# Strict decay sums on VectorE, and the chunk state from the pairing keys, in a bidirectional RWKV-7 recurrence

## The reference, cut to what matters

```python
def step(state, inp):
    r_t, w_t, k_t, v_t, a_t, b_t = inp
    sa = jnp.einsum('bhvk,bhk->bhv', state, a_t)
    state = state * w_t[:, :, None, :] + sa[..., None] * b_t[:, :, None, :] + v_t[..., None] * k_t[:, :, None, :]
    return state, jnp.einsum('bhvk,bhk->bhv', state, r_t)
```

## Time and profile before

| | |
|---|---|
| median of three runs | 1738.15 us (1738.0 to 1738.5) |
| profiled execution | span 1738.9 us from the first to the last instruction; no other time of it is given |
| TensorE busy | 1681.4 us (97%), weight loads 1105.9 us (64%) |
| VectorE, ScalarE, GpSimd busy | 837.8, 333.1 and 221.8 us |
| layer 1 and the mixing inputs | 0 to 589 us |
| prologue of the recurrence | 589 to 655.5 us, TensorE busy 64.1 of 66.5 |
| first turn (group 0, prepares 1) | 655.5 to 712.8 us, TensorE 54.8 of 57.3, VectorE 39.8, GpSimd 24.1 |
| second turn | 712.8 to 772.7 us, TensorE 54.8 of 59.9, VectorE 45.8, GpSimd 35.0 |
| third turn | 772.7 to 833.8 us, TensorE 56.2 of 61.1, VectorE 43.6, GpSimd 26.8 |
| last turn, output projection, router | 833.8 to 868 us |
| experts | 868 to 1738.9 us, TensorE 851 of 870.9, DMA 95% busy, 400 GB/s |

### The profile page before, as it was taken

One profiled execution on the slowest core, in us unless ns is written; L12 is line 12 of the kernel. 1 busy time (PEld: TensorE's weight loads), 2 busy tenths in 40 slices (PEclk: granted clock), 3 DMA queues, 4 the chain that ended last, 5 costly groups with the idle time before them and its releaser, 6 DMA issues.

```text
span 1738.9 us, 31942 instructions
## 1 busy us (share of the span) xinstructions
PE 1681.4 (97%) x13592; PEld 1105.9 (64%) x13592; DVE 837.8 (48%) x1889; ACT 333.1 (19%) x721; POOL 221.8 (13%) x301
## 2 busy tenths in 40 slices
PE   8999998999999999899899999999999999999997
PEld 5888886688644558788856555555555555555553
DVE  6666663555648446867335233433333333343332
ACT  3234323112101225444220000000101000000000
POOL 1431340000001423642300000000000000000000
PEclk9999999999999999999999999999999999999999
DMA  8542427454642010100686999999999999999996
GB/s 307 215 145 97 151 92 242 145 188 151 212 145 97 25 31 23 32 15 17 249 320 269 387 387 426 428 426 426 426 427 427 426 426 426 427 427 426 427 427 251
DMA packets 111553, 460.47 MB, mean 265 GB/s; under 512 B 28064, under 2 KB 57008, under 8 KB 89776
## 3 DMA queue, kind: packets, MB, share of 16 engines
q1 hardware_dynamic: 109360, 457.60, 66.4%
q10 hardware_dynamic: 2048, 0.78, 0.2%
HBM read 456.26 MB, written 2.10 MB: 264 GB/s over the span
## 4 chain that ended last, share of the span: by engine, by line
PE 87%; DMA 5%; DVE 4%; ACT 2%; issue 1%; SPq 1%; POOL 0%; DVEq 0%
PE ps L1658 20%; PE ps L845 15%; PE ps L1027 12%; PE ps L899 10%; PE ps L1631 10%; PE ps L1668 6%; DMA arena<-mw 4%; PE ps L1638 3%; PE ps L853 2%; PE ps L1195 2%; PE ps L891 1%; PE ps L1555 1%; PE ps L1041 1%; PE ps L919 1%; PE ps L1309 1%
## 5 line engine op out<-in xcount | busy, mean ns | idle before, releaser
L1658 PE MATMUL ps<-arena 128*64 128x256 f32 x3584 | 397.7, 380 | 5.3 <-DMA arena<-mw 5.3
L1658 PEld LDWEIGHTS ps<-arena 128*64 128x64 f32 x3584 | 256.7, 137 | 159.2 <-issue 30.7
L845 PE MATMUL ps<-arena 64*128 64x128 f32 (+13 forms) x1914 | 305.4, 329 | 15.2 <-DMA arena<-td 3.4
L2977 DVE TENSOR_TENSOR arena<-arena,ps 64x256 f32<-64x256 f32 x140 | 59.5, 425 | 460.0 <-ACT arena L2145 460.0
L845 PEld LDWEIGHTS ps<-arena 128*128 128x128 f32 (+4 forms) x1914 | 221.6, 187 | 83.2 <-issue 58.1
L1027 PE MATMUL ps<-arena 128*128 128x256 f32 x952 | 210.7, 379 | 0.1
L1631 PE MATMUL ps<-arena 128*64 128x512 f32 x896 | 203.0, 597 | 4.3 <-DMA arena<-mw 2.6
L1027 PEld LDWEIGHTS ps<-arena 128*128 128x128 f32 x952 | 178.5, 190 | 23.8 <-issue 0.5
L899 PE MATMUL ps<-arena 128*128 128x256 f32 (+1 forms) x714 | 189.0, 425 | 0.0
L2145 ACT ACTIVATE arena<-ps 64x256 f32<-64x256 f32 x140 | 52.7, 376 | 680.3 <-PE ps L1658 589.7
L899 PEld LDWEIGHTS ps<-arena 128*128 128x128 f32 x714 | 134.8, 190 | 50.6 <-issue 34.4
(11 more groups left out here) (288 smaller groups left out, 1377.9 us busy)
## 6 DMA issues: line engine op xcount, KB each, us to landing
arena<-mw SPq DMA_DIRECT2D x167, 2048.0 KB, 27.0
arena<-wqkv SPq DMA_DIRECT2D x35, 1024.0 KB, 7.3
arena<-fw SPq DMA_DIRECT2D x32, 1024.0 KB, 7.2
arena<-wrkv SPq DMA_DIRECT2D x12, 1024.0 KB, 7.4
arena<-awo SPq DMA_DIRECT2D x4, 1024.0 KB, 6.3
arena<-bwo SPq DMA_DIRECT2D x4, 1024.0 KB, 8.6
arena<-mw SPq DMA_DIRECT2D x2, 1024.0 KB, 38.6
arena<-rows SPq DMA_DIRECT2D x4, 384.0 KB, 4.8
```

The costliest lines, as they stand in the source:

```text
L845: last = mm(o, a, b, start=(n == 0), stop=(n == len(pairs) - 1))
L1658: last = mm(ps[r, g % 4, 0:256], picked[:, b, k, 0:64], w[:, k, a * 256:(a + 1) * 256], start=(k == 0), stop=(k == KB - 1))
L2977: dve.tensor_tensor(hid_e[RH:P, p % 2, i, :], sg_e[RH:P, j % 2, :], ps[RH:P, bank, 0:256], ALU.mult).then_inc(hide_sb, 1)
```

## The change

The full sums of both tiles come from one matmul of 128x512 per direction. The strict sums are the full ones minus `sig`: VectorE subtracts them (`strict_sums`) straight out of PSUM into `E[:, :, 1]`, and ScalarE takes their exponential in place in one operation (`strict_powers`). `powers` shrinks to two exponentials of 128x512 and the one of two columns. `ends`, `end_powers` and `to_end` are gone: `state` sums from the same scaled keys that the pairings use, and the factor that carries them to the chunk's end is now part of `pm`, whose two columns are each made by two matmuls of one column that add up. Since `state` reads these keys a turn later, the scaled keys alternate between two places, at the size that `keb` had. In VectorE's list of a turn `scaled_b` now stands ahead of `scaled_a`, and for direction 1 one step of the chain of the solve earlier; `scaled_a` of direction 1 stands one step later.

```diff
@@ -330,11 +330,11 @@
         cross = m.take(BLK // 2, BLK // 2)
-        keb0 = [m.take(2, RQ) for _ in range(2)]
+        spare_kt = [m.take(T, RQ) for _ in range(2)]
         b0 = m.take(T, RQ)
...
         b_ = [b0, m.take(T, RQ)]
-        keb = [keb0, [m.take(2, RQ) for _ in range(2)]]
+        spare_inv = [m.take(T, RQ) for _ in range(2)]
         y_sum = m.take(T, RQ)
@@ -359,6 +359,8 @@
             dirs.append(o)
+        k_at = [[o["kt"] for o in dirs], spare_kt]
+        b_at = [[o["inv"] for o in dirs], spare_inv]
         ar_early = [lent12.take(2, 2, P) for _ in range(2)]
@@ -779,7 +781,7 @@
             for d in range(2):
-                sp.wait_ge(ke_ok[d], 2 * NQ)
+                sp.wait_ge(ops_ok[d], 4 * NQ)
             for n in range(U_BWO):
@@ -1237,20 +1239,14 @@
             def cumulated(q, d):
+
                 pe.wait_ge(za.sb, q * 4 + 2 * d + 2)
-                cen = [const[:, C_CEN + (2 * d + n) * P:C_CEN + (2 * d + n + 1) * P] for n in range(2)]
-                for t in range(T):
-                    for n in range(2):
-                        last = run(ps[:, 2 * d + t, n * RQ:(n + 1) * RQ], [(cen[n], dirs[d]["sig"][:, t, :])])
-                last.then_inc(cum_ps, 1)
-
-            def ends(q, d):
-
                 sig = dirs[d]["sig"]
-                pe.wait_ge(ex_ok[d], q * 6 + 2)
-                run(ps[:, 2 * d, 0:RQ], [(tri(LS if d == 0 else US), sig[:, d, :])])
+                run(ps[:, 2 * d, :], [(const[:, C_CEN + 2 * d * P:C_CEN + (2 * d + 1) * P], sig.rearrange("p t n -> p (t n)"))]).then_inc(cum_ps, 1)
                 for pr in range(2):
-                    last = run(ps[:, 2 * d, RQ + pr:RQ + pr + 1], [(sig[:, 1 - d, pr * P:(pr + 1) * P], const[:, C_HALF + d:C_HALF + d + 1])])
+                    c = slice(pr * P, (pr + 1) * P)
+                    last = run(ps[:, 2 * d + 1, pr:pr + 1], [(sig[:, d, c], const[:, C_HALF + 1 - d:C_HALF + 2 - d]),
+                                                             (sig[:, 1 - d, c], const[:, C_HALF + d:C_HALF + d + 1])])
                 last.then_inc(end_ps, 1)
             def operands(q, i):
@@ -1259,10 +1255,10 @@
                 if i < 2:
-                    pe.wait_ge(ex_ok[i], q * 6 + 6)
+                    pe.wait_ge(ex_ok[i], q * 4 + 4)
                 else:
                     pe.wait_ge(X.sb, at_set(q, i - 2))
-                for done, bank, first, second in ((tA, b, o["E"][:, t, 1], o["E"][:, t, 0]), (tB, b + 1, o["inv"][:, t], o["kt"][:, t])):
+                for done, bank, first, second in ((tA, b, o["E"][:, t, 1], o["E"][:, t, 0]), (tB, b + 1, b_at[q % 2][d][:, t], k_at[q % 2][d][:, t])):
                     for pr in range(2):
@@ -1393,9 +1389,6 @@
                 four(z2, ETm[1], ze[1][0], RH)
-                if nq:
-                    ends(nq, 0)
-                    ends(nq, 1)
                 need(E2T, 0, 1)
@@ -1420,12 +1413,12 @@
                     for d in range(2):
-                        pe.wait_ge(ke_ok[d], 2 * (q + 1))
-                        k = keb[q % 2][d]
+                        pe.wait_ge(ops_ok[d], 4 * (q + 1))
+                        k, b = k_at[q % 2][d][:, d], b_at[q % 2][d][:, d]
                         for h in range(4):
...
                             at = (2 * d + h // 2) * RH
-                            last = run(ps[r, bank, at:at + RH], [(k[:, 0, c], value(q, d, h)), (k[:, 1, c], ze[d][0][:, h, :])])
+                            last = run(ps[r, bank, at:at + RH], [(k[:, c], value(q, d, h)), (b[:, c], ze[d][0][:, h, :])])
                     last.then_inc(St.ps, 1)
                 def keys_by_state(n, d):
@@ -1516,8 +1509,6 @@
             project(6)
-            ends(0, 0)
-            ends(0, 1)
             project(7)
@@ -1980,7 +1971,7 @@
                 if q:
-                    act.wait_ge(ke_ok[d], 2 * q)
+                    act.wait_ge(ops_ok[d], 4 * q)
                 for n, name in enumerate(("sig", "a")):
@@ -1988,15 +1979,17 @@
                 act.wait_ge(cum_ps, 2 * q + d + 1)
-                for t in range(T):
-                    act.activation(o["E"][:, t].rearrange("p a n -> p (a n)"), ps[:, 2 * d + t, :], ACT.Exp, scale=-DECAY).then_inc(ex_ok[d], 1)
-                    act.activation(o["inv"][:, t, :], ps[:, 2 * d + t, 0:RQ], ACT.Exp, scale=DECAY).then_inc(ex_ok[d], 1)
-
-            def end_powers(q, d):
-
+                sums = ps[:, 2 * d, :].rearrange("p (t n) -> p t n", t=T)
+                act.activation(b_at[q % 2][d], sums, ACT.Exp, scale=DECAY).then_inc(ex_ok[d], 1)
+                act.activation(o["E"][:, :, 0, :], sums, ACT.Exp, scale=-DECAY).then_inc(ex_ok[d], 1)
                 act.wait_ge(end_ps, 2 * q + d + 1)
-                act.activation(keb[q % 2][d][:, 1, :], ps[:, 2 * d, 0:RQ], ACT.Exp, scale=-DECAY).then_inc(ex_ok[d], 1)
-                act.activation(pm[q % 2][d], ps[:, 2 * d, RQ:RQ + 2], ACT.Exp, scale=-DECAY).then_inc(ex_ok[d], 1)
+                act.activation(pm[q % 2][d], ps[:, 2 * d + 1, 0:2], ACT.Exp, scale=-DECAY).then_inc(ex_ok[d], 1)
+
+            def strict_powers(q, d):
+
+                o = dirs[d]
+                act.wait_ge(excl_ok[d], q + 1)
+                act.activation(o["E"][:, :, 1, :], o["E"][:, :, 1, :], ACT.Exp, scale=-DECAY).then_inc(ex_ok[d], 1)
@@ -2048,9 +2041,9 @@
                 if nq:
+                    strict_powers(nq, 0)
                     powers(nq, 1)
-                    end_powers(nq, 0)
-                    end_powers(nq, 1)
+                    strict_powers(nq, 1)
                 at[0] = 12
@@ -2091,8 +2084,8 @@
             project_out(6)
-            end_powers(0, 0)
-            end_powers(0, 1)
+            strict_powers(0, 0)
+            strict_powers(0, 1)
             project_out(7)
@@ -2574,22 +2567,22 @@
             def scaled_a(q, d):
...
                 o = dirs[d]
-                dve.wait_ge(ex_ok[d], q * 6 + 4)
+                dve.wait_ge(ex_ok[d], q * 4 + 4)
                 dve.scalar_tensor_tensor(o["E"][:, :, 1, :], kkn, -1.0, o["E"][:, :, 1, :], ALU.mult, ALU.mult).then_inc(ops_ok[d], 1)
...
             def scaled_b(q, d):
+                o, b = dirs[d], b_at[q % 2][d]
+                dve.wait_ge(ex_ok[d], q * 4 + 1)
+                dve.tensor_tensor(k_at[q % 2][d], o["kd"], b, ALU.mult).then_inc(ops_ok[d], 1)
+                dve.tensor_tensor(b, o["a"], b, ALU.mult).then_inc(ops_ok[d], 1)
+
+            def strict_sums(q, d):
+
                 o = dirs[d]
-                dve.tensor_tensor(o["kt"], o["kd"], o["inv"], ALU.mult).then_inc(ops_ok[d], 1)
-                dve.tensor_tensor(o["inv"], o["a"], o["inv"], ALU.mult).then_inc(ops_ok[d], 1)
-
-            def to_end(q, d):
-
-                o, k = dirs[d], keb[q % 2][d]
-                dve.wait_ge(ex_ok[d], q * 6 + 6)
-                dve.tensor_tensor(k[:, 0, :], o["kd"][:, d, :], k[:, 1, :], ALU.mult).then_inc(ke_ok[d], 1)
-                dve.tensor_tensor(k[:, 1, :], o["a"][:, d, :], k[:, 1, :], ALU.mult).then_inc(ke_ok[d], 1)
+                dve.wait_ge(ex_ok[d], q * 4 + 2)
+                dve.tensor_tensor(o["E"][:, :, 1, :], ps[:, 2 * d, :].rearrange("p (t n) -> p t n", t=T), o["sig"], ALU.subtract).then_inc(excl_ok[d], 1)
@@ -2693,19 +2686,19 @@
                     keys(nq, 0)
-                    keys(nq, 1)
+                    key_rates(nq, 1)
+                    strict_sums(nq, 0)
+                    key_steps(nq, 1)
+                    scaled_b(nq, 0)
                     scaled_a(nq, 0)
-                    scaled_b(nq, 0)
                 chain_step(z2, 8, 0)
                 if nq:
-                    scaled_a(nq, 1)
+                    strict_sums(nq, 1)
+                    scaled_b(nq, 1)
                 chain_step(z3, 10, 0)
                 if nq:
-                    scaled_b(nq, 1)
+                    scaled_a(nq, 1)
                 chain_step(z5, 14, 0)
-                if nq:
-                    to_end(nq, 0)
-                    to_end(nq, 1)
                 dve.wait_ge(St.ps, q + 1)
@@ -2742,16 +2735,16 @@
             key_rates(0, 1)
+            strict_sums(0, 0)
+            strict_sums(0, 1)
             key_steps(0, 0)
+            scaled_b(0, 0)
             scaled_a(0, 0)
-            scaled_b(0, 0)
             key_steps(0, 1)
+            scaled_b(0, 1)
             scaled_a(0, 1)
-            scaled_b(0, 1)
             off_blocks(0, 0)
             off_blocks(0, 1)
-            to_end(0, 0)
-            to_end(0, 1)
             off_blocks(0, 2)
```

More of the change, by code:

```diff
@@ L464, in build @@
         ops_ok = [sem(f"ops_ok{d}") for d in range(2)]
-        ke_ok = [sem(f"ke_ok{d}") for d in range(2)]
+        excl_ok = [sem(f"excl_ok{d}") for d in range(2)]
         ex_ok = [sem(f"ex_ok{d}") for d in range(2)]
```

## The result

| | before | after |
|---|---|---|
| median, four runs each, same chip | 1738.33 us (1738.0 to 1741.33) | 1748.66 us (1747.74 to 1749.21) |
| ratio of the times, 95% interval | 1 | 1.0054 [1.0043, 1.0066] |
| span of the profiled execution | 1738.9 us | 1746.7 us |

A forecast was written before the change was run, and what follows sets the result against it. VectorE's list, stretched by GpSimd, was taken to bound z2 to z4 in two of three turns, TensorE elsewhere. Terms -1.4 + 0.4 + 3.9 + 3.4 = +6.3 us gave a 1744.5 us median, range 1738.5 to 1749 us.

The forecast's parts named there:

- stretched subtractions: Rival: in the second and third turn the subtraction and the extra operation cost 1.7 us each, not 0.6; 1748.9 us, chance 0.1.
- TensorE's savings: On TensorE, `cumulated` keeps its length and `ends` falls out: 1.77 us a turn, 7.1 us in all.
- Prologue: Before the first turn, the first transposes start earlier, limited by the scaled operands of direction 0; gain 1.4 us.
- First turn: z3 starts 0.9 us earlier, but work ahead of the z3 additions makes them 0.4 us later; net +0.4 us.
- z2 and z3 additions: VectorE, second and third turn: z2 additions 0.65 us late, z3 additions 1.95 us late; price 3.9 us for both turns.
- Stops and clock: Second and third turn: TensorE stops about 4.8 us before z3, 2 before z4; clock falls to half, 3.4 us more.
- eight exponentials: On ScalarE, eight exponentials of a direction's 1,794 columns become four of 1,538; the new wait costs nothing.
- Sum of the recurrence: Prologue, first turn, late additions and clock together: -1.4 + 0.4 + 3.9 + 3.4 = +6.3 us.
- The step that failed: Everything after the recurrence, the experts' weight stream included, only shifts with it, so the span becomes 1745.2 us.
- From span to median: The median lies 0.75 us below the profiled span of 1745.2 us, at 1744.5 us.
- late additions, but the clock holds: Rival: VectorE's additions come late in the second and third turn, but TensorE's clock stays up; 1740.5 us, chance 0.15.
- parts cancel: Rival: fewer late microseconds in the recurrence and half of the clock's price; 1738 to 1741.6 us, chance 0.1.

The follow-up runs named there:

- State_alone: The kernel before with only the change's second half (state from the pairing keys, no `ends` or `to_end`), strict sums still on TensorE; 1740.79 us, ratio 1.0009 to before.
- reorder_z2: The changed kernel with the chain's additions moved forward in VectorE's list, the z2 additions also ahead of the second subtraction; 1733.47 us, ratio 0.9972 to before.
- before_reorder: The kernel before with the chain's z2 and z3 additions moved forward in VectorE's list, old arithmetic kept; 1732.47 us, ratio 0.9954 to before.
- fill: The changed kernel with nine matmuls that compute nothing between z2 and z3 of the second and third turn; 1742.06 us, ratio 1.0017 to before.
- reorder_z2_pad: reorder_z2 plus 18 small matmuls that compute nothing and two waits in the last turn's TensorE stop; 1722.68 us, ratio 0.9901 to before.
- reorder: The changed kernel with the z2 and z3 additions moved forward in VectorE's list, behind both subtractions; 1735.77 us, ratio 0.9974 to before.

## Why the number was right and its reasons only in part

That the median fell into the range is luck. The recurrence was forecast 1.8 us too dear, the end of the execution was missing with 7.8 us, and the upper part of the range, in which 1748.66 us lies, had been opened for stretched subtractions, which did not come (0.68 us each).

- **TensorE's savings**: right. The two directions' `cumulated` with its paired one-column matmuls costs what it did (its one-column records take 240 ns from start to end, the unpaired ones took 229), `ends` is gone, and TensorE is busy 6.0 us less, forecast 7.1; the matmuls at the lower clock count longer.
- **Prologue**: forecast -1.4 us, measured -1.39. By the rows named, 608.10 and 606.57, it would have been 1.5.
- **First turn**: forecast +0.4, measured +0.17.
- **z2 and z3 additions**: forecast 0.65 and 1.95 us late, measured 0.34 and 1.76, both counted from the turn's start in the second turn; 1.76 in the third too. It was the first operation of `scaled_b` that met GpSimd's (1.56 us), not the second (0.68).
- **Stops and clock**: 4.67 and 1.28 us for the forecast 4.8 and 2; the clock at 1.2 GHz behind them, in both turns. Its price is the turn's 3.01 us less the 1.76, 1.25 us, in the second turn (forecast 2.0) and 2.71 - 1.76 = 0.95 us in the third (forecast 1.4). State_alone's second turn, where the clock fell and the additions came on time, shows 2.1 us.
- **ScalarE**: the "eight exponentials" of a direction are six, four in `powers` and two in `end_powers`; nothing hung on it.
- **Sum of the recurrence**: forecast +6.3 us, measured -1.39 + 0.17 + 3.01 + 2.71 = +4.5, the lateness 3.5 (forecast 3.9) and the clock 2.2 (forecast 3.4).
- **The step that failed**: the sum adds up the recurrence and then says "All that follows, the start of the experts' weight stream too, moves with the recurrence." What lies behind the last matmul was put at nothing by this, and it grew by 7.8 us, more than the whole recurrence, for a reason outside it: TensorE's queue drains 13.3 us behind its last matmul, not 4.4. For the stretch up to the last projection the sentence stands, within the 2 us by which single executions scatter. Together the two parts make 12.3 us beside the 10.3 us of the medians; the 2 us between them are of the size of that scatter, and no run explains them.
- **From span to median**: the forecast put the median 0.75 us below the span, but 1738.15 and 1738.9 us belong to different executions. The time lies 1.8 to 2.0 us above the span of the same execution, so a median of 1744.5 us goes with a span of about 1742.6 (an estimate), not 1745.2.
- **Without the late end** the change would stand at 1748.66 - 7.8 = 1740.9 us, an estimate from the two spans, some 2.5 us or 0.15% above before: nearest to the rival "late additions, but the clock holds" (1740.5 us) in its number, though the clock did fall, and within "parts cancel".
- **Whether the arithmetic is worth it**: with the additions moved forward and TensorE's stream padded, the changed arithmetic runs at 0.9901 [0.9881, 0.9921]; the old one's best is 0.9954 [0.9942, 0.9966]. A part of that gap is the filled stop in the last turn, which the old arithmetic could have too; that was not tried, so the gap is not the arithmetic's alone. The turns alone speak for the changed arithmetic: 56.05, 55.98 and 56.54 us in reorder_z2 against 57.25, 57.27 and 57.48 in before_reorder, 3.4 us together.

## What to carry to other kernels

Before a difference of some microseconds is explained by the edited stage, lay the same landmarks side by side from the first to the last instruction, the drains at the end included; here the turns' lateness was taken for the cause through eleven runs because the sizes fitted. Ask too how far each stretch scatters between executions of other kernels before a single difference is given a reason. An experiment that changes the number of instructions can change the end too, so compare it with a control of the same length, or subtract the time behind the last transfer. A stop of TensorE that can't be removed can be filled with matmuls that compute nothing, where dense work follows: in fill and in reorder_z2_pad the matmuls behind the filled stop ran at the full clock (1.15 us in place of 1.98, 3.83 in place of 5.45).

## What the runs showed of the hardware

- TensorE's queue can end up to 8.9 us later than usual behind its last matmul (13.3 against 4.4 us) with three more instruction loads running there. It goes with TensorE's code and not with the work: six kernels of 13560 records have it, eight of four other lengths have not, and 18 matmuls and two waits more took it away. Whether the length decides or the place of the code, by which rule, and whether the loads serve TensorE, stays open.
- Side by side, VectorE and GpSimd stretch each other's operations. Of VectorE's operations of 128x512 that read only SBUF, one takes 1.2 to 1.8 us beside GpSimd and 0.68 alone; in fill it was GpSimd's that were stretched (1.37 for 1.04 us). One that reads PSUM takes 0.68 us, and inserting one shortens the next SBUF operation from 1.44 to 0.72 us. The Trainium skill, "GPSIMD Engine Reference", section Specifications, says that GpSimd's SBUF interfaces are shared with VectorE, with contention for instructions of two SBUF inputs. By that rule the stretched rows are the ones with two SBUF operands, and the traces agree: 1.44 to 1.75 us against 0.68 for the subtraction, which has one.
- A stop of 2.09 us left the clock at 2.4 GHz once and ones of 2.07 and 2.05 us (state_alone) did not; behind 4.67 and 4.51 us it was down each time. In reorder it fell to 1.2 GHz behind a stop of 1.56 us in the second turn and stayed at 2.4 GHz behind one of 1.57 us in the third. The length of one stop does not decide alone.
